# 160 tokens on gathered expert rows instead of 128, and tiles of u loaded in pairs

## The reference, cut to what matters

```python
def peer_ffn(h, w_query, sub_keys, expert_u, expert_v):
    q = (xt @ w_query).reshape(n, PEER_HEADS, 2, PEER_DKEY // 2)
    s = jnp.einsum('nhmd,mkd->nhmk', q, sub_keys)
    ...   # top 16 of each half, top 16 of the 256 sums: eidx (n, 8, 16), softmax gate
        act = jax.nn.gelu(jnp.einsum('nd,nhkd->nhk', x_blk, expert_u[i_blk]))
        return jnp.einsum('nhk,nhkd->nd', g_blk * act, expert_v[i_blk])
```

## Time and profile before

| | us |
|---|---|
| median of 3 runs (5053.87 to 5058.83) | 5057.36 |
| the profiled execution | 5058.33 |
| its span, first to last instruction | 5056.5 |
| dense products with u, 2027 to 3552 | 1525 |
| of it the row stretch, 2831 to 3552 | 721 |
| values, 3581 to 4765 | 1184 |

### The profile page before, as it was taken

The page is one execution under the profiler, slowest core; times in us unless marked ns, Lnnn a source line. Parts: engine busy times, 40 slices in busy tenths (PEclk is TensorE's granted clock), DMA queues, the critical chain, the costliest instruction groups (busy, mean ns, idle before and its releaser), DMA issues. The chain is left out here.

```text
span 5056.5 us, 81549 instructions
## 1 busy us (share of the span) xinstructions
PE 4658.0 (92%) x28870; PEld 4380.5 (87%) x28870; DVE 2405.3 (48%) x4197; ACT 1594.9 (32%) x2480; POOL 2472.8 (49%) x1773
## 2 busy tenths in 40 slices
PE   5999985999679979899999999999799999999879
PEld 4888874888349979899999999999799999999779
DVE  3366643554132110578677444444465565566421
ACT  3222222444133322322355333333233333333222
POOL 4677730233014433345444577777455665665333
PEclk8999985999779989999999999999899999999989
DMA  3233311333954342233455799999677777777333
GB/s 96 72 90 89 88 44 40 101 114 90 374 219 129 127 151 74 77 94 112 124 183 183 258 329 331 327 331 325 249 276 267 277 271 280 266 276 278 126 93 97
DMA packets 351235, 926.14 MB, mean 183 GB/s; under 512 B 41426, under 2 KB 118738, under 8 KB 300146
## 3 DMA queue, kind: packets, MB, share of 16 engines
q1 hardware_dynamic: 279090, 570.86, 35.2%
q0 software_dynamic: 37872, 272.25, 14.0%
q10 hardware_dynamic: 34128, 81.15, 4.3%
HBM read 838.12 MB, written 86.02 MB: 183 GB/s over the span
## 5 line engine op out<-in xcount | busy, mean ns | idle before, releaser
L2479 PE MATMUL val_y_ps<-val_wt,val_v 128*128 128x416 f32 x6144 | 1183.5, 353 | 29.2 <-POOL val_v L2464 29.2
L2479 PEld LDWEIGHTS val_y_ps<-val_wt,val_v 128*128 128x128 f32 x6144 | 1141.6, 188 | 71.1 <-issue 29.5
L243 PE MATMUL rt_acc<-xn_act,rt_w_hi 128*128 128x416 f32 x4096 | 1122.8, 355 | 17.2 <-POOL rt_w_rest L233 16.6
L233 POOL TENSOR_TENSOR rt_w_rest<-rt_w_raw,rt_w_hi 128x512 fp32r<-128x512 f32 x576 | 743.1, 1306 | 657.1 <-ACT rt_w_hi L228 651.8
L2464 POOL TENSOR_TENSOR val_v<-val_v_raw,val_v 128x2048 fp32r<-128x2048 f32 x128 | 592.0, 4625 | 464.1 <-ACT val_v L2510 464.1
L243 PEld LDWEIGHTS rt_acc<-xn_act,rt_w_hi 128*128 128x128 f32 x4096 | 757.7, 188 | 36.0 <-POOL rt_w_rest L233 27.2
L243 PE MATMUL rt_acc<-xn_act,rt_w_rest 128*128 128x416 f32 x2048 | 714.5, 349 | 0.0
L2560 DVE TENSOR_TENSOR out_xT<-out_xT,val_y_ps 128x416 f32<-128x416 f32 x512 | 299.7, 585 | 488.4 <-PE val_y_ps L2479 451.5
L228 ACT ACTIVATE rt_w_hi<-rt_w_raw 128x512 fp32r<-128x512 f32 x576 | 348.7, 630 | 529.7 <-DMA rt_w_raw<-in_peer_uT 357.8
L2386 DVE CUSTOM_DVE_ANT_0 rt_space<-rt_space,rt_mid 128x2048 f32<-128x2048 f32 x128 | 292.8, 2287 | 425.8 <-DMA rt_space<-in_peer_u,out_row_id 425.8
L2510 ACT ACTIVATE val_v<-val_v_raw 128x2048 fp32r<-128x2048 f32 x128 | 245.7, 1920 | 625.7 <-PE val_y_ps L2479 624.9
(11 more groups left out here) (395 smaller groups left out, 7361.9 us busy)
## 6 DMA issues: line engine op xcount, KB each, us to landing
rt_w_raw<-in_peer_uT SPq DMA_DIRECT2D x512, 256.0 KB
val_v_raw<-in_peer_vp SPq DMA_DIRECT2D x128, 1024.0 KB, 4.9
scan_w_raw<-in_w_in SPq DMA_DIRECT2D x128, 256.0 KB, 2.9
pages_K<-in_cache_kT SPq DMA_DIRECT2D x64, 512.0 KB
pages_V<-in_cache_v SPq DMA_DIRECT2D x64, 512.0 KB, 12.3
hid_scratch<-rt_hid ACTq DMA_DIRECT2D x128, 208.0 KB
gate_scratch<-rt_space ACTq DMA_DIRECT2D x13, 2048.0 KB, 7.3
val_hid<-hid_scratch SPq DMA_DIRECT2D x32, 832.0 KB
```

Source lines behind the costliest of these rows:

```text
L233: e.tensor_tensor(self.rest[:, s, 0:nk, :], self.raw[:, s, 0:nk, :], self.hi[:, s, 0:nk, :].bitcast(F32), ALU.subtract).then_inc(self.rest ...
L243: mm = e.matmul(acc[:, h, 0:width], w[:, s, k, :], act[:, kt0 + k, a, col + h * width:col + (h + 1) * width], start=first and k == 0 and w ...
L2479: mm = e.matmul(y_ps[:, t % 2, 0:DW], v[:, c % 2, a, j, t * P:(t + 1) * P], wt[:, g % 2, j, b, :], start=j == 0 and a == 0 and b == 0, sto ...
```

## The change

32 more tokens (`EX`) take their experts by rows, so `DW` falls from 416 to 384, the gate chunks from 13 to 12 and the gate stretch from 26 to 24 blocks; the row stretch grows from 77 to 79 blocks. The 32 tokens' 128 picks are laid as four groups of 32 partitions with 32 picks each (`XK`), so that 32 more indirect DMAs bring them: 160 (`NR`) in all. Their ids and gates go to their partitions by 8 small DMAs, issued by ScalarE at the start of the gate stretch. For them TensorE transposes the activations a second time, after 32 of the 39 pairs of blocks of the row stretch.

The gathered rows of u have six places instead of three (the third waits for the last gate store), the rows of v four instead of three. From block 8 on, u is loaded two units at a time, 4 KB a partition instead of 2 KB, into half of the ring, when both units there are split. In `stage_values` the 128 first rows are spread over parts 0 to 103 and the other 32 over parts 104 to 127, so that 32 parts have two rows. Between them ScalarE copies the first sum out (`keep_rows`). The transposes and adds of the first 128 tokens move into the last group; after it 16 small matmuls with `stack` sum the four partition groups.

```diff
--- before.py
+++ after.py
@@ -50,10 +50,14 @@
 LAM_INIT = 0.2
 NEG = -1e30
 TB = 5
-D0, DN, DW = P, 1, TOK - P
-DTOK = DN * DW
+EX = 32
+D0 = P + EX
+DW = TOK - D0
+DTOK = DW
 HK = NH * TOPK
-ROWS = 3
+XK = HK * EX // P
+NR = HK + XK
+ROWS = 4
 CH, BT, Q = 32, 8, 4
 GR = 4
 VW = 512
...
-    def split_hi(self, e, i, per, u, nk=UNIT):
+    def load_two(self, e, i, per, u, src):
+
+        e.wait_ge(self.rest_done, i * per + (u + 2))
         s = u % RING
-        e.wait_ge(self.landed[s], i * (16 * (per // RING)) + 16 * (u // RING + 1))
+        e.dma_start(self.raw[:, s:s + 2].rearrange("p s k c -> p (s k) c"), src).then_inc(self.landed[s], 16)
+
+    def split_hi(self, e, i, per, u, nk=UNIT, two=False):
+        s = u % RING
+        e.wait_ge(self.landed[s - s % 2 if two else s], i * (16 * (per // RING)) + 16 * (u // RING + 1))
         e.wait_ge(self.used, i * per + (u + 1))
         e.activation(self.hi[:, s, 0:nk, :], self.raw[:, s, 0:nk, :], ACT.Copy).then_inc(self.hi_done, 1)
 
...
+        spot = space[:].rearrange("p (r n) -> p r n", n=D_MODEL)
+        xn2 = spot[:, 4, :].rearrange("p (j n) -> p j n", j=KT)
+        SPOTS = (5, 6, 0, 1, 2, 3)
+        IN_OUT = 2
...
+        def row(n):
+
+            return spot[:, SPOTS[n % len(SPOTS)], :]
...
             with e.Fori(0, (PK - T_A) // 2) as i:
-                for u in range(2 * U):
-                    w.load(e, i, 2 * U, base(T_A) + u, columns(k.peer_uT, i * 2 + (T_A + u // U), UNIT * (u % U)))
+                for u in range(0, 2 * U, 2):
+                    w.load_two(e, i, 2 * U, base(T_A) + u,
+                               columns(k.peer_uT, i * 2 + (T_A + u // U), UNIT * (u % U), 2 * UNIT))
...
-                    if n < HK and n * (T_D - 1) * U < HK * ((t - FIRST_D) * U + u + 1):
-                        if n >= ROWS:
-                            e.wait_ge(row_dot, n - ROWS + 1)
-                        e.indirect_dma_start(row[:, n % ROWS, :], None, k.peer_u,
+                    if n < NR and n * (T_D - 1) * U < NR * ((t - FIRST_D) * U + u + 1):
+                        if n >= len(SPOTS):
+                            e.wait_ge(row_dot, n - len(SPOTS) + 1)
+                        if n == IN_OUT:
+                            for a in range(2):
+                                e.wait_ge(gates_stored[a], 16 * (NCH // 2 + 1))
+                        if n == HK:
+                            e.wait_ge(more_in, 2 * 16 * (P // EX))
+                        e.indirect_dma_start(row(n), None, k.peer_u,
                                              bass.IndirectOffsetOnAxis(ap=k.row_id[:, n:n + 1], axis=0)
-                                             ).then_inc(rows_in[n % ROWS], 16)
+                                             ).then_inc(rows_in[n % len(SPOTS)], 16)
                         n += 1
                     w.split_rest(e, 0, 0, base(t) + u)
...
+            e.wait_ge(ids_ready, 1)
+            for g in range(P // EX):
+                r, c = slice(g * EX, (g + 1) * EX), slice(g * XK, (g + 1) * XK)
+                e.dma_start(k.row_id[r, HK:NR], more_id[:, c]).then_inc(more_in, 16)
+                e.dma_start(k.row_gate[r, HK:NR], more_gate[:, c]).then_inc(more_in, 16)
             for u in range(2):
-                w.split_hi(e, 0, 0, base(FIRST_C) + u)
+                w.split_hi(e, 0, 0, base(FIRST_C) + u, two=True)
...
-            chunk(NCH // 2, 0)
...
                 for u in range(2 * U):
-                    w.split_hi(e, i, 2 * U, base(FIRST_D) + u + 2)
+                    w.split_hi(e, i, 2 * U, base(FIRST_D) + u + 2, two=True)
...
-            chunk(NCH // 2, 0)
-
-            with e.Fori(0, (T_D - 1) // 2) as i:
+
+            def pair(i):
                 for j in range(2):
                     e.wait_ge(acc_free, i * 2 + (FIRST_D + j))
                     part(i, 2 * U, base(FIRST_D) + j * U, j, range(U))
+
+            TURN = -(-HK * (T_D - 1) // NR // 2)
+            with e.Fori(0, TURN) as i:
+                pair(i)
+            e.wait_ge(xn2_ready, 1)
+            e.wait_ge(row_dot, HK)
+            for j in range(KT):
+                mm = e.transpose(mid[:, j // 4, (j % 4) * P:(j % 4 + 1) * P], xn2[:, j, :], k.c("ident"))
+            mm.then_inc(xn_turned, 1)
+            with e.Fori(TURN, (T_D - 1) // 2) as i:
+                pair(i)
...
+            ch.did(e.tensor_copy(k.row_gate[:, 0:HK], rows[:, 2, 0, :]))
+            ch.did(e.tensor_copy(more_gate[:], rows[0:EX, 2, 1, :]))
+            ch.step(e.tensor_scalar(pick_id[:], rows[:, 0, 0:2, :], float(PK), None, ALU.mult))
+            ch.step(e.tensor_tensor(pick_id[:], pick_id[:], rows[:, 1, 0:2, :], ALU.add))
+            ch.did(e.tensor_copy(k.row_id[:, 0:HK], pick_id[:, 0, :]))
+            ch.step(e.tensor_copy(more_id[:], pick_id[0:EX, 1, :]))
...
+            e.wait_ge(ps_ready, 2 * BT // Q + NCH * GROUPS)
+            more = [k.act[:, :, a, P:P + EX].bitcast(F32).unsqueeze(2).broadcast_to([P, KT, P // EX, EX])
+                    for a in range(2)]
+            e.tensor_tensor(xn2.rearrange("p j (g n) -> p j g n", n=EX), more[0], more[1], ALU.add).then_inc(xn2_ready, 1)
+            for t in range(NR):
+                if t == HK:
+                    e.wait_ge(xn_turned, 2)
+                e.wait_ge(rows_in[t % len(SPOTS)], 16 * (t // len(SPOTS) + 1))
...
-        def groups(e, part):
-            with e.Fori(0, NG // 2 - 1) as i:
+        TURN = NG * HK // NR // 2 + 1
+        FIRST = 2 * TURN * NC
+
+        def groups(e, part, between=lambda: None):
+            with e.Fori(0, TURN) as i:
+                part(i, 0, True, True)
+                part(i, 1, True, True)
+            between()
+            with e.Fori(TURN, NG // 2 - 1) as i:
                 part(i, 0, True, True)
                 part(i, 1, True, True)
             part(NG // 2 - 1, 0, True, False)
             part(NG // 2 - 1, 1, False, False)
+
+        def rows_of(t):
+
+            if t < FIRST:
+                return range(-(-t * HK // FIRST), -(-(t + 1) * HK // FIRST))
+            last = NG * NC - FIRST
+            return range(HK - (-(t - FIRST) * XK // last), HK - (-(t + 1 - FIRST) * XK // last))
...
+            for t in range(NG * NC):
+                for n in rows_of(t):
+                    if n >= ROWS:
+                        e.wait_ge(row_done, n - ROWS + 1)
+                    e.indirect_dma_start(rows[:, n % ROWS, :], None, k.peer_v,
+                                         bass.IndirectOffsetOnAxis(ap=k.row_id[:, n:n + 1], axis=0)
+                                         ).then_inc(rows_in[n % ROWS], 16)
...
+            def turn(a):
+
+                if a >= 2:
+                    e.wait_ge(row_added, a - 1)
+                for t in range(4 * a, 4 * a + 4):
+                    mm = e.transpose(act_ps[:, a % 2, (t % 4) * P:(t % 4 + 1) * P], row_out[:, t * P:(t + 1) * P],
+                                     k.c("ident"))
+                mm.then_inc(row_turned, 1)
+
             def part(i, g, more, ahead):
                 e.wait_ge(w_rest, at(i, g, GR, 3 * GR))
                 for c in range(NC):
+                    if not more and c in (1, 3):
+                        turn(c - 1)
+                        turn(c)
...
-            e.wait_ge(row_out_done, 1)
+            e.wait_ge(row_out_done, 2)
+            e.wait_ge(row_added, 4)
             for t in range(KT):
...
+                mm = e.matmul(act_ps[:, 0, t * EX:(t + 1) * EX], row_out[:, t * P:(t + 1) * P], k.c("stack"),
+                              start=True, stop=True)
+            mm.then_inc(row_turned, 1)
...
+            def keep_rows():
+                e.wait_ge(row_done, HK)
+                e.activation(row_out[:], row_ps[:], ACT.Copy).then_inc(row_out_done, 1)
+
+            groups(e, part, keep_rows)
+            e.wait_ge(row_done, NR)
+            e.wait_ge(row_turned, 4)
             e.activation(row_out[:], row_ps[:], ACT.Copy).then_inc(row_out_done, 1)
...
+                if t == HK:
+                    e.wait_ge(row_out_done, 1)
+                if t in (0, HK):
+                    e.tensor_scalar(row_ps[:], rows[:, t % ROWS, :], row_w[:, t:t + 1], None,
+                                    ALU.mult).then_inc(row_done, 1)
...
-                    row(g * NC + c)
+                    for n in rows_of(g * NC + c):
+                        row(n)
+                    if g == NG - 1 and c in (0, 2):
+                        for a in range(c, c + 2):
+                            e.wait_ge(row_turned, a + 1)
+                            x = k.xT[:, 4 * a:4 * a + 4, 0:P]
+                            e.tensor_tensor(x, x, act_ps[:, a % 2, :].rearrange("p (a n) -> p a n", a=4),
+                                            ALU.add).then_inc(row_added, 1)
...
+            e.wait_ge(row_turned, 5)
+            x = k.xT[:, :, P:P + EX]
+            e.tensor_tensor(x, x, act_ps[:, 0, :].rearrange("p (a n) -> p a n", n=EX), ALU.add).then_inc(row_added, 1)
```

## The result

The changed kernel takes 5215.55 us (median of four runs, 5210.81 to 5216.91), the kernel before on the same chip 5058.09 (5053.87 to 5068.83). The ratio is 1.0306, 95% interval 1.0288 to 1.0324: 157 us slower, where 5035 was predicted, 22 us faster. It lies outside the range of 4985 to 5105.

A forecast was written before the change was run, and what follows sets the result against it. The prediction took matmuls to bound the gate stretch and values, and TensorE and the DMAs both to be near their limits in the row stretch. -55.6 + 5 + 28 = -22.6 us gave 5035, range 4985 to 5105.

The forecast's parts named there:

- Pitch: Time per matmul: 384 columns should take 174.9 ns, 14.1 less than the 189.0 at 416 columns.
- Query, ranking and gate stretches: The stretches before the row stretch: narrower matmuls and fewer gate blocks save time, 55.6 us less in all.
- Row stretch: The stretch of dense products with u: 79 blocks x 9.0 + 15 = 726 us against 721, +5.
- I take 9.0: Row stretch: us a block after the change, chosen between 8.85 and 9.66, with TensorE wanting 8.55.
- the dear price: DMA cost of gathered rows as in the row stretch before: 2.86 us a row, 9.04 a block summed.
- the cheap one: DMA cost of gathered rows as in the values: 2.37 us a MB, 2.49 a row, 8.28 a block summed.
- Rival (c): Row stretch: pair loads starve the ring; landing + 3.85, 10.15 us a block, +96 there, 5126 in all; chance 0.12.
- Values: The values stretch: 1200 us for parts and second rows, 12 for `keep_rows`; 1212 against 1184, +28.
- Tail: After the last part: fewer transposes and adds (-2), 4 adds and 16 transposes more (+2), so nothing.
- (b): Row stretch: DMAs full at this stretch's price, 9.66 us a block, +57 there, 5087 in all; chance 0.18.
- (d): Values: second rows of v cost less than said, up to -75 us, 4960 at best; chance 0.08.
- (a): Row stretch: DMAs follow TensorE fully, 8.55 us a block at 403 GB/s, -31 there, 4999 in all; chance 0.20.

## Why the prediction was wrong

**Pitch: right.** 50 us with 287 matmuls are 174.2 ns, 174.9 predicted.

**Query, ranking and gate stretches: -48, not -55.6.** The first two take 459 instead of 473 (-14, -16.9 predicted), the gate stretch 296 instead of 331 (-35; -38.7 with the small DMAs). Of the gap, 3 us are those DMAs: ScalarE's issues took 0.61 each, not the 0.34 of the store in the earlier trace rows, and its first high part came 5.68 us late instead of 2.7. The other 4 or 5 us were not traced. The lines:

```profile
2485.48 0.62 ACTq L2168 DMA_DIRECT2D out_row_id<-rt_more_id  x1
2486.13 0.60 ACTq L2169 DMA_DIRECT2D out_row_gate<-rt_more_gate  x1
...
2490.68 2.19 ACT L238 ACTIVATE rt_w_hi<-rt_w_raw 128x512 fp32r<-128x512 f32 x4 [5.68 <-issue]
```

**Row stretch: the step that failed.** The term "I take 9.0" was 10.85, outside the 8.5 to 9.7 beyond which the prediction called itself wrong, and +146 of the 180 by which the sum missed. The step priced each queue's bytes, added them up and divided by the share that was reached, 0.936. That assumes that the DMA engines were the limit and 0.936 their ceiling. Neither holds. The share reached 1.01 at 402 GB/s with eight slots. Nor is there a fixed price. The queues of the changed kernel from 2860 to 3430, and that of u in the run without rows of u:

```profile
q0 software_dynamic: 15556, 113.29, 53.7%
q1 hardware_dynamic: 15126, 55.08, 29.2%
...
q1 hardware_dynamic: 19378, 70.53, 37.1%
```

With four slots rows cost 0.537 x 570 / 113.29 = 2.70 us a MB, the dear price (2.73), though the 2 KB pieces were gone; with eight slots 0.623 x 570 / 145.06 = 2.45, near the cheap one (2.37). The 4 KB pieces of u cost 3.02 with four slots, 3.00 without the rows of u beside them and 2.59 with eight slots, where the engines moved most. So the time that packets took was no fixed price that could be added up to a block's time. What the prediction read as two resources close to their limits was a loop with a latency in it: load a slot, wait until it lands, split it, load again. The share of 0.95 and ScalarE's long wait for u fit both readings, and the next wait, ScalarE's 334 us, was put down to the DMAs' throughput, where it was their latency over four slots. The kernel before with eight slots shows it: 702 instead of 721, at a DMA share that is no higher.

Rival (c) had the mechanism, its formula (landing + 3.85) and the picture in the profile. Its landing was taken at 6.3 and was 6.9 to 7.0, its splits 3.8 to 3.9, as said; and it got 0.12 because 1 MB of v lands in 4.8 us. That row is of the values, at a share of 0.71, and 256 KB in the row stretch took 6 to 8 us. The landing should have been taken from the stretch in question. With 6.9 the sum would have been 79 x 10.75 + 15 - 721 = +143, near the measured +151. The half-ring wait cost the other stretches nothing, as said: with unit loads all of the gain was in the row stretch. At the entry ScalarE stood 11.8 us for u, and the second transposes cost nothing to be seen.

By the Trainium skill ("DMA: Bandwidth & Descriptors", Specifications) HBM gives a core about 358 GB/s. This case's runs speak against it as a limit for the one core that runs here: 402 GB/s, reads and writes together, over 570 us.

**Values: +51, not +28.** A part with one row 8.75 (8.79), one with two +2.43 (+2.35), the stop behind `keep_rows` 11.3 (12). 96 x 8.75 + 32 x 11.18 + 11.3 = 1209, against 1212 predicted. What was left out is the clock: the 25 us that the windows sum up to. The working took each stall at its own length and the matmuls behind it at full speed. With the stalls gone the low clock is gone too: the values of the run with rows and `keep_rows` moved have no window of 2 us below 0.9. Between the two lies the run that moved the rows alone. It keeps a stop behind `keep_rows`, of 7.1 us, and its clock falls there and nowhere else in the values, for 2 us in the same sum. Of the 31 stops of 2.6 us in the changed kernel 17 passed without a fall; what decides it was not tried.

**Tail: +2, not 0.** The 16 matmuls with `stack` stand in the profile as 32 of 220 ns one after another, against four groups of four transposes that took turns with VectorE's adds:

```profile
4925.02 7.04 PE L2556 MATMUL val_act_ps<-all_const,val_row_out 128*128 128x32 f32 x32 [4.82 <-ACT val_row_out L2595]
```

Rivals (b) and (d) fall: the DMAs were not full, and the second rows cost what was said. (a) was what the change can do once the ring lets it.

## What to carry to other kernels

Take a ring of n slots, each refilled once it has been worked off. If a load lands after L and the work on a slot takes w, the ring delivers at most n slots per L + w, however much bandwidth is left. Compute this bound, with L read under the load of that stretch, before pricing any bytes. Joining two loads into one halves the number of places that are refilled on their own, so it takes more slots to keep the loads as far ahead; here the larger pieces brought nothing, and in the kernel before the lost depth cost 103 us. And when a second helping of work is put at a point where an engine already holds the next one up, first move that work to where it is covered: moving the rows from the end of a part into its middle made the values 139 us shorter.

## What the runs showed of the hardware that was not expected

- The DMA engines moved 402 GB/s for 570 us from three queues at once (gathered 8 KB rows, 2 or 4 KB pieces of u, stores), at a share of 1.01 by the profile. A share of 0.95 was no proof that they were full.
- The time that packets of one kind took changed with the rest: 4 KB pieces of u 3.00 to 3.02 us of the 16 engines a MB at 147 and 313 GB/s in all, 2.59 at 402; gathered rows 2.70 and 2.45.
- A 512 KB load landed in 3.7 us (3.5 to 3.9) at 147 GB/s on the queues, and in some 6.9 beside two rows a block (from the last split to the next high part, at 313 GB/s); one of 256 KB beside them took 6.7 (3.8 to 10.0), at 353. Under load, half the size did not land in half the time.
- After 14 of 31 stops of TensorE of 2.6 us, full before and behind, the granted clock was 0.50 to 0.78 in the next windows of 2 us, then 1.00; with the stop of 11.3 us that is 25 us in the values. The other 17 passed without it (the part at 4025).
- Small DMAs over 32 partitions took ScalarE 0.61 us each to issue, the stores of sums 0.34.
